# Unrotated scores of the latent attention from high and low halves: three one-record products in place of one of full operands

## Chip, cores and metric

One core of one Trainium2 chip. The metric is the device time of one execution in microseconds; the figure for the kernel before is the median of three runs. Times inside an execution are from one profiled execution.

## The reference

Two blocks in a row, in float32, on 512 tokens of width 2048. The first is a windowed attention block with sinks; the change does not touch it. The second puts 16 meta tokens ahead (528 keys), projects the normed tokens and runs two attentions, one differential (8 heads) and one latent (8 heads), gates both and projects back. The latent one is what the change touches:

```python
q_nope, q_pe = qB[..., :B_NOPE], _rope(qB[..., B_NOPE:], pos)      # 128 unrotated, 64 rotated
k_nope, vB = kvB[..., :B_NOPE], kvB[..., B_NOPE:]
s = (einsum('bhqd,bhkd->bhqk', qn, k_nope) + einsum('bhqd,bkd->bhqk', qp, k_pe)) * scale
s = where(rel >= 0, s, -inf);  p = softmax(s)
o = einsum('bhqk,bhkd->bhqd', p, v)
```

## The kernel before, in words

The kernel is written by hand, one instruction stream for each engine, synchronized by counting semaphores. Its backbone is a series of projections ("chunks"): 512 tokens (4 tiles of 128) times 16 blocks of 128 rows of a weight, 512 columns wide. A chunk has 64 steps; step Q is the product of token tile t = Q % 4 with weight block k = Q // 4. Both operands are split: a value x is held as hi (rounded to float32r) and lo = x - hi, also float32r, and one product is hi·hi + hi·lo + lo·hi, three matmuls of 512 columns (L601 to L603). A float32r matmul leaves one record in the trace; one of plain float32 operands leaves two. ScalarE makes the high half of each weight block (L1061), GpSimd the low half (L1559); SyncE loads the weights.

The attentions are interleaved with the steps of four chunks. The function attend_body (for TensorE at L947, ScalarE L1421, VectorE L2117; GpSimd's is attend_loads, L1685) says for each step Q what an engine issues besides the projection; the order of the work is written out by these step numbers, the same on each engine. Chunks 26 and 27 carry the latent attention (object MLA), four heads each; chunks 28 and 29 carry the differential one (DIFF). A head has four units, one for each 128 queries; unit u stands at step unit_time(u) = 12 + 3u (L441). Tile j of a head sees (j + 1)·128 + 16 keys: 144, 272, 400, 528, the last in two cuts of 272 and 256 because of the PSUM bank.

For a latent head, in the order of its work:

- GpSimd loads its q, k and v (load_qk L1645, load_v L1660) into one of two buffers. VectorE rotates the 64 rotated columns of q in place (rotate L2021) at step 12·head - 3, for head 0 at step 4.
- head_turn (L874) transposes at three steps, given by turn_time (L445): b = 0 the unrotated q, b = 1 the rotated q (with 64 unrotated columns beside it), b = 2 the unrotated k. All three go into the one PSUM bank turn[0], the 16 meta keys into turn[1]. For heads 1 to 3 the steps are 12·head + 2, + 5 and + 7; for head 0 they are 6, 8 and 10. b = 0 waits for the rotation.
- keep_head (L1376) on ScalarE copies them out: q to qnT (L1382, times the scale, float32), k to knT (L1388, L1390, float32); of the rotated q the high half to the upper 64 partitions of qpT (L1385). Of the latter VectorE writes the low half to the lower 64 partitions (L2134), so that one float32r product against a doubled k covers both halves.
- scores2 (L902) at the unit's step: for each cut, one product of qnT and knT in float32 (L917), then qpT against kpeT_hi and against kpeT_lo in float32r (L919, L920), all into the same PSUM region.
- soften2 (VectorE, L2086) adds the mask and takes the maximum in the same step; weigh2 (ScalarE, L1393) takes the exponential one step later; combine (VectorE, L2100) the reciprocal at + 2; turn_p2 (TensorE, L923) transposes p into turn[0] at + 3 (L929, L931); keep_pT2 (ScalarE, L1399) copies that out; values2 (TensorE, L934) at + 5 multiplies with v (L943, L944) into turn[1]; keep_o2 (VectorE, L2111) scales it out at + 5.

Who may write turn[0] is counted: each use (three turns and four p's a head) waits in t0_use (L897) until the semaphore A.free has as many releases as uses went before. The instruction that last reads the bank adds one: L1382 for b = 0, L2134 for b = 1, L1390 for b = 2, the end of keep_pT2 for p. values2 of the latent attention waits for all releases of the uses so far:

```python
pe.wait_ge(A.free, i * (4 * A.batches + NU) + ((count["t0"] if A.mla else turned_at[u]) + 1))
```

Within a step TensorE issues first the projection, then values2, head_turn, scores2, turn_p2. ScalarE: the weight split (each fourth step), weigh2, keep_head, keep_pT2. VectorE: keep_o2, combine, the rotation, the low half of q, soften2. Each queue is in order.

## Time and profile before

| What | Value |
|---|---|
| Median of three runs | 1683.43 us (1682.55 to 1684.44) |
| The profiled execution's own time | 1682.62 us |
| Its span, first to last instruction | 1680.8 us |
| Mean granted TensorE clock | 0.999 |
| TensorE busy | 1666.2 us (99%), 8383 matmul records |
| VectorE, ScalarE, GpSimd busy | 695.9 us (41%), 784.3 us (47%), 707.4 us (42%) |
| The two latent bodies | from 1048 to 1218 us |

Busy of TensorE counts from the start of a matmul to its modelled end, and matmuls are pipelined, so rows overlap; the distance between two starts is what a matmul takes of the engine. PE is TensorE, PEld its weight loads, DVE VectorE, ACT ScalarE, POOL GpSimd. The chain of waits follows the execution back from its last instruction to what released each step.

### The profile page before, as it was taken

How to read it: one execution, taken by the hardware profiler on the slowest of the kernel's cores; microseconds unless marked ns; L12 is line 12 of the kernel's file. 1: busy time of each engine (PE TensorE's matmuls, PEld its weight loads, DVE VectorE, ACT ScalarE, POOL GpSimd, SP SyncE). 2: the span in 40 equal slices, each digit the busy share in tenths (PEclk: the TensorE clock that was granted, in tenths of full speed). 3: DMA queues.
4: the chain of work that ended last, by engine and by line, in shares of the span. 5: the costliest groups of instructions: out<-in, count | busy, mean ns of one | idle time of the engine just before them, and what ended most of it. 6: DMA issues, size and time to landing. Idle time of an engine off the chain costs nothing.

```text
span 1680.8 us, 22142 instructions
## 1 busy us (share of the span) xinstructions
PE 1666.2 (99%) x8383; PEld 1367.0 (81%) x8383; DVE 695.9 (41%) x1696; ACT 784.3 (47%) x1699; POOL 707.4 (42%) x569
## 2 busy tenths in 40 slices
PE   9999999999999999999999999999999999999998
PEld 7889898888888888898887787888866767888886
DVE  4356656663135666231100001423234344767574
ACT  4356666664334455442312236444455555434551
POOL 4442433225666304455455544434333333665022
PEclk9999999999999999999999999999999999999999
DMA  6341444214886577433677676423332212324772
GB/s 228 115 125 51 128 84 116 76 56 125 195 182 145 168 237 252 142 122 125 129 209 190 181 195 224 144 93 120 104 114 89 95 51 76 99 79 142 237 245 100
DMA packets 118374, 234.81 MB, mean 140 GB/s; under 512 B 8475, under 2 KB 16220, under 8 KB 118124
## 3 DMA queue, kind: packets, MB, share of 16 engines
q1 hardware_dynamic: 78332, 147.70, 26.6%
q0 software_dynamic: 18352, 48.15, 13.9%
q10 hardware_dynamic: 21584, 37.55, 6.9%
q8 instruction: 67, 1.10, 0.3%
q14 instruction: 39, 0.32, 0.1%
HBM read 208.41 MB, written 58.51 MB: 159 GB/s over the span
## 4 chain that ended last, share of the span: by engine, by line
PE 94%; DVE 3%; issue 1%; ACT 1%; POOL 1%; DMA 0%; DVEq 0%; ACTq 0%; POOLq 0%
PE acc L601 21%; PE acc L603 20%; PE acc L602 20%; PE sc L917 4%; PE turn L698 3%; PE turn L943 2%; PE turn L623 2%; PE turn L686 1%; PE acc L741 1%; PE acc L742 1%; PE acc L743 1%; PE sc L614 1%; PE sc L615 1%; PE turn L931 1%; PE sc L673 1%
## 5 line engine op out<-in xcount | busy, mean ns | idle before, releaser
L1559 POOL TENSOR_TENSOR w_lo<-w_raw,w_hi 128x512 fp32r<-128x512 f32 x405 | 584.9, 1450 | 886.2 <-ACT w_hi L1061 875.8
L1061 ACT ACTIVATE w_hi<-w_raw 128x512 fp32r<-128x512 f32 x517 | 323.3, 628 | 497.3 <-PE acc L603 403.6
L601 PE MATMUL acc<-w_hi,setA_hi 128*128 128x512 f32 (+1 forms) x1344 | 544.2, 405 | 2.5 <-DVE setA_lo L1744 0.8
L603 PE MATMUL acc<-w_hi,setA_lo 128*128 128x512 f32 (+1 forms) x1344 | 521.0, 388 | 0.0
L602 PE MATMUL acc<-w_lo,setA_hi 128*128 128x512 f32 (+1 forms) x1344 | 519.6, 387 | 0.0
L601 PEld LDWEIGHTS acc<-w_hi,setA_hi 128*128 128x128 f32 x1344 | 252.8, 188 | 57.2 <-issue 11.7
L603 PEld LDWEIGHTS acc<-w_hi,setA_lo 128*128 128x128 f32 x1344 | 252.2, 188 | 53.0
L602 PEld LDWEIGHTS acc<-w_lo,setA_hi 128*128 128x128 f32 x1344 | 253.4, 189 | 40.0
L1912 DVE TENSOR_TENSOR w_lo<-w_raw,w_hi 128x512 fp32r<-128x512 f32 x112 | 78.7, 708 | 64.0 <-ACT w_hi L1061 63.9
L2016 DVE TENSOR_TENSOR sum_m<-sc,tmp_m 16x512 f32<-16x512 f32 (+1 forms) x9 | 5.9, 656 | 230.1 <-ACT tmp_m L1081 230.1
L1137 ACT ACTIVATE p_w<-sm,negm 128x256 f32<-128x256 f32 (+1 forms) x128 | 60.6, 474 | 57.1 <-DVE sink_d L1814 57.1
L1396 ACT ACTIVATE p<-sm,negm 128x144 f32<-128x144 f32 (+3 forms) x96 | 54.3, 566 | 53.5 <-DVE negm L2097 53.5
L917 PE MATMUL sc<-knT,qnT 64*128 64x272 f32 (+6 forms) x240 | 77.7, 415 | 0.8 <-DVE negm L2097 0.4
L601 PE MATMUL acc<-w_hi,setB_hi 128*128 128x512 f32 x192 | 76.7, 399 | 0.0
L603 PE MATMUL acc<-w_hi,setB_lo 128*128 128x512 f32 x192 | 75.0, 391 | 0.0
L602 PE MATMUL acc<-w_lo,setB_hi 128*128 128x512 f32 x192 | 74.8, 390 | 0.0
L1404 ACT ACTIVATE pT<-turn 128x128 f32<-128x128 f32 (+1 forms) x64 | 28.0, 437 | 91.7 <-PE turn L931 91.7
L698 PEld LDWEIGHTS turn<-vg,pT 128*128 128x128 f32 x448 | 59.9, 191 | 5.3
L917 PEld LDWEIGHTS sc<-knT,qnT 64*128 64x128 f32 (+1 forms) x240 | 39.3, 186 | 22.0 <-DVE negm L2097 13.0
L698 PE MATMUL turn<-vg,pT 128*128 128x64 f32 x448 | 56.9, 267 | 0.0
L2115 DVE TENSOR_SCALAR o_nat<-turn,rden 128x128 f32<-128x128 f32 x64 | 22.4, 349 | 81.3 <-PE turn L944 81.3
L1810 DVE CUSTOM_DVE_ANT_0 sm<-sc,bias,sink_g 128x256 f32<-128x256 f32 (+1 forms) x128 | 52.5, 447 | 0.1
(391 smaller groups left out, 2546.1 us busy)
## 6 DMA issues: line engine op xcount, KB each, us to landing
w_raw<-in_w_in SPq DMA_DIRECT2D x48, 1024.0 KB, 5.1
w_raw<-in_swa_w_in SPq DMA_DIRECT2D x35, 1024.0 KB, 7.5
w_raw<-sum_out SPq DMA_DIRECT2D x64, 256.0 KB, 3.8
sum_out<-in_swa_w_out POOLq DMA_DIRECT2D x24, 512.0 KB, 7.8
sum_out<-in_w_out POOLq DMA_DIRECT2D x24, 512.0 KB, 7.8
sum_out<-sum_out POOLq DMA_DIRECT2D x16, 512.0 KB, 6.7
w_raw<-in_swa_w_out SPq DMA_DIRECT2D x8, 1024.0 KB, 5.3
w_raw<-in_swa_w_out SPq DMA_DIRECT2D x24, 256.0 KB, 3.9
```

Source lines behind the costliest of these rows:

```text
L601: mm(acc[t][:, 0:cols], hi[:, kc, rows], wh, start=(k == 0), stop=False)
L602: mm(acc[t][:, 0:cols], hi[:, kc, rows], wl, start=False, stop=False)
L603: last = mm(acc[t][:, 0:cols], lo[:, kc, rows], wh, start=False, stop=(k == K - 1))
L623: last = nc.tensor.transpose(turn[bank][:, t * P:(t + 1) * P], tile, ident[:])
L698: last = mm(o_ps[:, h * HD:(h + 1) * HD], pT[:, u % 2, 2 * h + c], vg[:, j - 1 + c], start=(c == (1 if j == 0 else 0)), stop=(c == 1))
L917: last = mm(dst, qnT[rows, buf, q], knT[rows, buf, keys], start=True, stop=not A.mla)
L1061: nc.scalar.activation(w_at(f)[0], raw_of(f), ACT.Copy).then_inc(done, 1)
L1137: nc.scalar.activation(p_w[:, u % 2, h, first:], sm[:, u % 2, h, first:], ACT.Exp, bias=negm[:, u % 2, h:h + 1], scale=-1.0, accum_out=den ...
L1396: nc.scalar.activation(p2[:, u % 2, comp, lo:], sm2[:, slot, lo:], ACT.Exp, bias=negm_2[:, u % 2, comp:comp + 1], scale=-1.0, accum_out=de ...
L1559: nc.gpsimd.tensor_tensor(lo, raw_of(f), hi.bitcast(F32), ALU.subtract).then_inc(s_lo, 1)
L1810: last = V.tensor_tensor_reduce(sm[:, u % 2, h, first:], sc[h][:, first:256], bias[:, head, first:], -1.0, sink_g[:, head:head + 1], ALU.a ...
L1912: V.tensor_tensor(lo, raw_of(f), hi.bitcast(F32), ALU.subtract).then_inc(s_wlo, 1)
```

## The change

The unrotated q and k are no longer kept as float32 but as a high and a low half in float32r. ScalarE's copies (the same number of them) now write the high halves; VectorE writes the low halves by subtraction from PSUM, and it is VectorE that now releases turn[0] after b = 0 and b = 2. Each score cut has three float32r products for the unrotated part where it had one float32 product. The low halves lie in a part of SBUF that nothing uses at that time (qn_lo at B_LO, kn_lo behind it). For head 0 the turns stand at steps 4, 7, 10; b = 0 waits for the loads alone, and b = 1 for the rotation. The differential attention's part of the code is only rewritten.

```diff
@@ -209,8 +209,12 @@
         gate_0 = over("gate_0", [P, NT, CW], B_HI)
         nat_k = over("nat_k", [P, 2, NT, VD], B_HI + 6144)
         nat_v = over("nat_v", [P, 2, NT, VD], B_HI + 10240)
+        qn_hi = over("qn_hi", [P, 2, S], B_HI + 14336, F32R)
+        qn_lo = over("qn_lo", [P, 2, S], B_LO, F32R)
+        qpT = over("qpT", [P, 2, S], B_HI + 18432, F32R)
+        kn_hi = over("kn_hi", [P, 2, KEYS], B_HI + 22528, F32R)
+        kn_lo = over("kn_lo", [P, 2, KEYS], B_LO + 4096, F32R)
         qnT = over("qnT", [P, 2, S], B_HI + 14336)
-        qpT = over("qpT", [P, 2, S], B_HI + 18432, F32R)
         knT = over("knT", [P, 2, KEYS], B_HI + 22528)
         alibi = over("alibi", [P, ALIBI_AT[NT]], B_HI + 26752)
         kpeT_lo = over("kpeT_lo", [P, KEYS], B_HI + 29952, F32R)
@@ -312,7 +316,7 @@
         s_short = [sem(f"s_short{i}") for i in range(2)]
         s_st, s_gld, s_zero = sem("s_st"), sem("s_gld"), sem("s_zero")
         s_lam, s_alibi, s_fin_w, s_x1in, s_h2, s_fin = (sem("s_" + n) for n in ("lam", "alibi", "fin_w", "x1in", "h2", "fin"))
-        s_qp_hi = sem("s_qp_hi")
+        s_qp_hi, s_qn_hi, s_kn_hi = sem("s_qp_hi"), sem("s_qn_hi"), sem("s_kn_hi")
         s_km_in, s_km_ps, s_km = sem("s_km_in"), sem("s_km_ps"), sem("s_km")
         s_sum, s_sq, s_fin_last, s_x1last = sem("s_sum"), sem("s_sq"), sem("s_fin_last"), sem("s_x1last")
 
@@ -445,7 +449,7 @@
         def turn_time(A, head, b):
 
             if head == 0:
-                return 6 + 2 * b if A.mla else 5 + 3 * b
+                return 4 + 3 * b if A.mla else 5 + 3 * b
             return 12 * head + ((2, 5, 7)[b] if A.mla else (5, 8)[b])
 
         def score_at(A, u, comp):
@@ -875,7 +879,9 @@
 
                 buf, use = head % 2, i * 2 + (head // 2 + 1)
                 if b == 0:
-                    pe.wait_ge(A.rope if A.mla else A.ld_qk[buf], i * 4 + (head + 1) if A.mla else use * 32)
+                    pe.wait_ge(A.ld_qk[buf], use * (48 if A.mla else 32))
+                if A.mla and b == 1:
+                    pe.wait_ge(MLA.rope, i * 4 + (head + 1))
                 t0_use(A, i)
                 if b == A.batches - 1:
                     if A.mla:
@@ -914,8 +920,12 @@
                 for first, end in zip(cuts, cuts[1:]):
                     keys = slice(first, end)
                     dst = sc2[:, start + keys.start:start + keys.stop]
-                    last = mm(dst, qnT[rows, buf, q], knT[rows, buf, keys], start=True, stop=not A.mla)
-                    if A.mla:
+                    if not A.mla:
+                        last = mm(dst, qnT[rows, buf, q], knT[rows, buf, keys], start=True, stop=True)
+                    else:
+                        mm(dst, qn_hi[:, buf, q], kn_hi[:, buf, keys], start=True, stop=False)
+                        mm(dst, qn_lo[:, buf, q], kn_hi[:, buf, keys], start=False, stop=False)
+                        mm(dst, qn_hi[:, buf, q], kn_lo[:, buf, keys], start=False, stop=False)
                         mm(dst, qpT[:, buf, q], kpeT_hi[:, keys], start=False, stop=False)
                         last = mm(dst, qpT[:, buf, q], kpeT_lo[:, keys], start=False, stop=True)
                 last.then_inc(A.score, 1)
@@ -1377,18 +1387,22 @@
                 buf = head % 2
                 act.wait_ge(A.full, i * (4 * A.batches + NU) + (count["t0"] + 1))
                 count["t0"] += 1
-                scale = B_SCALE if A.mla else A_SCALE
+                if A.mla:
+                    if b == 0:
+                        nc.scalar.activation(qn_hi[:, buf], turn[0][:], ACT.Copy, scale=B_SCALE).then_inc(s_qn_hi, 1)
+                    elif b == 1:
+                        nc.scalar.activation(qpT[ROPE:P, buf], turn[0][ROPE:P, :], ACT.Copy, scale=B_SCALE).then_inc(s_qp_hi, 1)
+                    else:
+                        nc.scalar.activation(kn_hi[:, buf, META:KEYS], turn[0][:], ACT.Copy)
+                        nc.scalar.activation(kn_hi[:, buf, 0:META], turn[1][:, 0:META], ACT.Copy).then_inc(s_kn_hi, 1)
+                    return
                 if b == 0:
-                    last = nc.scalar.activation(qnT[:, buf], turn[0][:], ACT.Copy, scale=scale)
-                elif b < A.batches - 1:
-
-                    nc.scalar.activation(qpT[ROPE:P, buf], turn[0][ROPE:P, :], ACT.Copy, scale=scale).then_inc(s_qp_hi, 1)
-                    return
+                    last = nc.scalar.activation(qnT[:, buf], turn[0][:], ACT.Copy, scale=A_SCALE)
                 else:
+                    n = 4 * i + head
                     nc.scalar.activation(knT[:, buf, META:KEYS], turn[0][:], ACT.Copy)
-                    meta = turn[1][:, 0:META] if A.mla else diff_kmT[:, (4 * i + head) * META:(4 * i + head + 1) * META]
-                    last = nc.scalar.activation(knT[:, buf, 0:META], meta, ACT.Copy)
-                last.then_inc(A.free, 1)
+                    last = nc.scalar.activation(knT[:, buf, 0:META], diff_kmT[:, n * META:(n + 1) * META], ACT.Copy)
+                last.then_inc(DIFF.free, 1)
 
             def weigh2(A, i, u, comp):
                 lo, slot = S - (u % NT + 1) * P, u % 2 if A.mla else comp
@@ -2129,6 +2143,16 @@
                             x1, x2_ = nat_q[:, buf, :, VD:VD + HR], nat_q[:, buf, :, VD + HR:QB]
                             rotate((x1, x2_), (x1, x2_), cos[:], sin[:], [rope_t[:, n] for n in range(4)]).then_inc(MLA.rope, 1)
                             dve.wait_ge(MLA.rope, i * 4 + (head + 1))
+                        if A.mla and Q == turn_time(A, head, 0):
+                            dve.wait_ge(s_qn_hi, i * 4 + (head + 1))
+                            V.scalar_tensor_tensor(qn_lo[:, head % 2], turn[0][:], B_SCALE, qn_hi[:, head % 2].bitcast(F32),
+                                                   ALU.mult, ALU.subtract).then_inc(MLA.free, 1)
+                        if A.mla and Q == turn_time(A, head, 2):
+                            dve.wait_ge(s_kn_hi, i * 4 + (head + 1))
+                            V.tensor_tensor(kn_lo[:, head % 2, 0:META], turn[1][:, 0:META],
+                                            kn_hi[:, head % 2, 0:META].bitcast(F32), ALU.subtract)
+                            V.tensor_tensor(kn_lo[:, head % 2, META:KEYS], turn[0][:],
+                                            kn_hi[:, head % 2, META:KEYS].bitcast(F32), ALU.subtract).then_inc(MLA.free, 1)
                         if A.mla and Q == turn_time(A, head, 1):
                             dve.wait_ge(s_qp_hi, i * 4 + (head + 1))
                             V.scalar_tensor_tensor(qpT[0:ROPE, head % 2], turn[0][ROPE:P, :], B_SCALE,
```

## Rows read from the trace of the kernel before

**Rows 1.** Chain by engine; windows view: us, busy PE, PEld, DVE, ACT, POOL (count), PEclk, DMA, GB/s

```profile
PE 94%; DVE 3%; issue 1%; ACT 1%; POOL 1%; DMA 0%; DVEq 0%; ACTq 0%; POOLq 0%
...
1048.00:1218.00 170.00, 169.82 (x986) 142.27 (x985) 52.33 (x220) 75.78 (x202) 70.38 (x77) 1.00 0.36 114
```

**Rows 2.** Timeline of TensorE: start us, us, engine line op out<-in; scores of four widths

```profile
1066.47 0.83 PE L917 MATMUL sc<-knT,qnT 128*128 128x400 f32 x2
...
1067.33 0.34 PE L920 MATMUL sc<-kpeT_lo,qpT 128*128 128x400 f32 x1
1067.51 0.27 PE L929 MATMUL turn<-ident,p 128*16 128x128 f32 x1
...
1071.67 0.62 PE L917 MATMUL sc<-knT,qnT 128*128 128x272 f32 x2
...
1072.25 0.28 PE L920 MATMUL sc<-kpeT_lo,qpT 128*128 128x272 f32 x1
1072.37 0.59 PE L917 MATMUL sc<-knT,qnT 128*128 128x256 f32 x2
...
1072.92 0.29 PE L920 MATMUL sc<-kpeT_lo,qpT 128*128 128x256 f32 x1
1073.05 0.27 PE L929 MATMUL turn<-ident,p 128*16 128x128 f32 x1
...
1076.47 0.41 PE L917 MATMUL sc<-knT,qnT 128*128 128x144 f32 x2
...
1076.78 0.27 PE L920 MATMUL sc<-kpeT_lo,qpT 128*128 128x144 f32 x1
1076.89 0.27 PE L929 MATMUL turn<-ident,p 128*16 128x128 f32 x1
```

**Rows 3.** Waits view, 1048 to 1218 us: us in total, times, longest us

```profile
PEld turn L943 <- ACT knT L1390: 1.8, 6, 0.3
...
PEld turn L884 <- DVE qpT L2134: 1.0, 2, 0.5
```

**Rows 4.** Timeline after b2 of head 2, first body

```profile
1088.44 0.18 ACT L1390 ACTIVATE knT<-turn 128x16 f32<-128x16 f32 x1
...
1088.67 0.41 PEld L943 LDWEIGHTS turn<-nat_v,pT 128*128 128x128 f32 x3 [0.30 <-ACT knT L1390]
```

**Rows 5.** Timeline after b0 and after b1 of head 2, first body

```profile
1080.57 0.60 ACT L1382 ACTIVATE qnT<-turn 128x512 f32<-128x512 f32 x1 [1.79 <-PE turn L889]
1081.78 0.27 PE L929 MATMUL turn<-ident,p 128*16 128x128 f32 x1
...
1084.46 0.59 ACT L1385 ACTIVATE qpT<-turn 64x512 fp32r<-64x512 f32 x1 [0.81 <-PE turn L892]
1085.15 0.69 DVE L2134 SCALAR_TENSOR_TENSOR qpT<-turn,qpT 64x512 fp32r<-64x512 f32 x1 [0.71 <-ACT qpT L1385]
1085.99 0.27 PE L929 MATMUL turn<-ident,p 128*16 128x128 f32 x1
```

**Rows 6.** Groups by line: busy us, mean ns; timeline of VectorE, head 1's rotation

```profile
L1794 DVE TENSOR_TENSOR kT_lo<-turn,kT_hi 128x512 fp32r<-128x512 f32 x4 | 2.7, 677 | 0.0
...
L2059 DVE TENSOR_TENSOR kpeT_lo<-sc,kpeT_hi 64x16 fp32r<-64x16 f32 x2 | 0.3, 156 | 0.0
...
1059.46 0.29 DVE L2028 TENSOR_TENSOR nat_q<-rope_t 128x128 f32<-128x128 f32 x1
1059.67 0.28 DVE L2029 TENSOR_TENSOR nat_q<-rope_t 128x128 f32<-128x128 f32 x1
```

**Rows 7.** Source view of L884: duration ns min/median/max

```profile
L884 PE MATMUL turn<-ident,nat_k x64: 270/273/330, 1057.4 to 1382.1; 128*128 128x128 f32 x64
```

**Rows 8.** Timeline of head 0, first body, to its first scores

```profile
1057.66 1.36 DVE L2025 TENSOR_TENSOR rope_t<-nat_q,sin 128x128 f32<-128x128 f32 x1
...
1058.70 0.18 ACT L1390 ACTIVATE knT<-turn 128x16 f32<-128x16 f32 x1
...
1059.60 0.41 PE L917 MATMUL sc<-knT,qnT 128*128 128x144 f32 x2
```

## The prediction

> **What bounds the kernel now.** I read the chain of waits first: TensorE holds 94% of it [rows 1]. The windows view of the stretch that the change touches, the two latent-attention bodies (chunks 26 and 27, 1048 to 1218 us), shows TensorE busy for 169.8 of 170 us at the full clock, VectorE for 52, ScalarE for 76 [rows 1]. So each nanosecond of TensorE issue time there counts, and so does each wait in TensorE's in-order queue; work on VectorE or ScalarE costs nothing by itself, but where TensorE waits for its result it does. A matmul row's duration includes its drain, so a product costs the distance from its start to the next start. I took that from the timeline. Then I read the waits view and the timeline around the turns of a head, to find who waits for the one bank turn[0].
>
> Below, step +n is projection step 12·head+n of a body. With heads 1 to 3 the bank turn[0] is used in this order: p turned (+0), q unrotated (+2, "b0"), p (+3), q rotated (+5, "b1"), p (+6), k (+7, "b2"), p (+9). Values run at +5, +8 and so on. In the latent bodies values2 (L940) waits for as many releases as turn[0] has had uses, so the values at +8 wait for the release of b2.
>
> **The scores.** A full-operand product shows as two records, a one-record product as one. All distances are start to start, up to L929 or the next L917 [rows 2].
> - 144 keys: five records' unit takes 1076.47 to 1076.89 = 0.42 us, the last one-record product 0.11. Five one-record products: 0.55, so +0.13.
> - 272 keys: 1071.67 to 1072.37 = 0.70; one product 0.12; five 0.60, so -0.10. It occurs twice in a head (tile 1, and the first cut of tile 3).
> - 256 keys: 0.68; one product 0.13 by this row, five 0.65 at most; I take -0.06.
> - 400 keys: 1066.47 to 1067.51 = 1.04; one product 0.18; five 0.90, so -0.14.
> A head: 0.13 - 0.10 - 0.14 - 0.10 - 0.06 = -0.27. Eight heads: **-2.2 us**. The gain is small because at 144 keys a one-record product takes 0.11 us where its 144 columns are 0.06 at 2.4 GHz, the granted level there [rows 1]: I read it as the three products paying for their weight loads, which the long full-operand product hid.
> The Trainium skill says in FP8 and Floating Point Precision, TensorE Precision Notes, that true FP32 is 4 passes through the array. By that alone one pass over 1344 keys a head is saved, 0.56 us, or 4.5 us in all, an estimate; the 272 and 400 rows are near it, the 144 row is against it and decides here.
>
> **b2, the turn of k.** Now ScalarE copies k (L1388, L1390) and releases the bank; TensorE waits for precisely this: the waits view has 6 waits of the value products for L1390 [rows 3]. In the timeline L1390 ends at 1088.44 + 0.18 = 1088.62 and the weight load of L943 starts at 1088.67, 0.05 later [rows 4]. After the change the same two ScalarE copies write the high half, then VectorE makes two subtractions, and the last one releases. Added: 0.10 from the end of a ScalarE copy to VectorE's start (L1385 ends at 1085.05, L2134 starts at 1085.15 [rows 5]); the 16-column subtraction, 0.16 long, of which 0.07 lies under its successor, as with L2028 and L2029 (0.29 long, starts 0.21 apart): 0.09; and the 512-column one from PSUM, 0.68 [rows 6]. Sum 0.87, bounds 0.78 (the small one free) to 0.95. TensorE already waits there, so all of it lands on the path: 6 x 0.87 = **+5.2 us**. Behind the subtraction in VectorE's queue stand keep_o2 and combine of step +8, which need the delayed values anyway.
>
> **b0, the turn of q unrotated.** Now L1382 ends at 1080.57 + 0.60 = 1081.17 and L929 of the p turned at +3 starts at 1081.78, so there is 0.61 of cover [rows 5]. After: 1081.17 + 0.10 + 0.69 (as L2134, same shape of operation on 64 rows) = 1081.96, and 0.05 to TensorE: 1082.01. The scores before it are 0.10 shorter, so L929 would be due at 1081.68. Wait 0.33, and a first transpose after a wait takes 0.06 more (330 against 273 ns [rows 7]): 0.39 x 6 = **+2.3 us**. Bounds: 0.23 (if the shorter scores count for nothing and the restart is free) to 0.5.
>
> **b1, the turn of q rotated.** Nothing is added, but its cover shrinks. L2134 ends at 1085.84, TensorE could go on at 1085.89; L929, now at 1085.99, would be due at 1085.85 with the 400-key scores 0.14 shorter [rows 5]. 0.04 + 0.06 = 0.10, six times: **+0.6 us**. So most of the 400-key gain is given back.
>
> **Head 0 of each body.** The turns move from steps 6, 8, 10 to 4, 7, 10; b0 no longer waits for the rotation, which b1 does. The loads landed before the rotation that ran ahead of step 6, and three steps of some 0.7 us between turns cover the longer chain. The wait of b2 for L2134 goes (1.0 us over 2 by the load side's idle time [rows 3]). In its place comes a later k: the scores at step 12 now start at 1059.60, after L1390 ends at 1058.88 [rows 8]. After: in VectorE's queue the rotation of head 1 (step 9) stands ahead of k's subtraction (step 10). It ends at 1059.67 + 0.28 = 1059.95 [rows 6]; everything up to it comes a step earlier, 1059.25; then 0.05 + 0.09 + 0.68 and 0.05: 1060.12, that is +0.5. In that rotation one operation, L2025, took 1.36 us where its like take 0.28 [rows 6, 8]; without that the result is about nothing. I take +0.25 each, **+0.5 us** (-0.1 to +1.1).
>
> Nothing else is on the path. ScalarE runs as many copies as before, of the same lengths. VectorE gets three more subtractions a head, some 1.5 us against 118 idle; POOL only waits longer before it loads a head that is used 12 steps on. No transfer is added.
>
> **Sum.** -2.2 + 5.2 + 2.3 + 0.6 + 0.5 = +6.4 us. The profiled execution took 1682.62 us (span 1680.8 and 1.8 around it) and would become 1689.0. It lies 0.8 under the median of the runs; on the median 1683.43 + 6.4 = **1689.8 us**.
>
> **Rivals.**
> 1. *The release is hidden*: turn[0]'s subtraction runs under projection steps, as it does for head 0's b1, and TensorE's waits do not grow. For: VectorE is two thirds idle. Against: the 6 waits for L1390, and cover of 0.61 against a chain of 0.84 at b0. It decides at the values of step +8: if they don't wait for k's low half, 5.2 goes and 1684.6 is left; if b0 is covered as well, 1681.7. Not slower. Chance 0.10.
> 2. *A whole pass is saved*: every full-operand product costs four passes and every one-record product one, also at 144 keys, by a weight load that is hidden. Then -4.5 in place of -2.2, with the waits as above: 1687.5. This is the page's rule named above. Against: 0.11 us steps of one-record products at 144 keys. Chance 0.04; together with rival 1 (1683.4 - 4.5 = 1678.9, faster) 0.03.
> 3. *Knock-on*: VectorE's queue, which now holds the subtractions with their waits for ScalarE, delays the softmax of the next unit, mostly where the rotation (up to 1.4 us long in one operation) follows at +9, and p comes late to its turn. 6 x 0.7 = 4 us more: 1694. Against: the unit's turn is three steps, over 3 us, behind its scores. Chance 0.08.
> The forecast keeps 0.75.
>
> **Range and chances.** The bounds of b2 (±0.5), b0 (-1.0, +0.7), head 0 (±0.6), the scores (-2.3 by rival 2) and of the runs' own spread give 1686.3 to 1692.8; rival 1 and most of rival 3 stay out. About 0.2% (3.4 us) can be told from no change here. Faster needs rivals 1 and 2 together: 0.03. Within 0.2%: rival 1 and its kin, 0.12. Slower: 0.85.
>
> **What would show it.** In the waits view of the changed kernel: 6 waits of value products (L943's successor) for the subtraction that makes kn_lo, each about 0.9 us longer than the 6 for L1390 now; 6 of the turned p at +3 for qn_lo, about 0.35 each; 2 at step 12 for kn_lo. The four tile widths should show 0.55, 0.60, 0.90 and 1.2 to 1.25 us in scores. If the value products at +8 start as early as now, the forecast is wrong at its largest term. If one-record products of 144 keys step at 0.06, the second term is wrong.

## The result, and the profile after

The changed kernel took 1692.24 us (median of 5 runs, 1691.63 to 1692.85) against 1683.43 for the kernel before (1682.52 to 1684.61): a ratio of 1.0054 [1.0043, 1.0065], so 0.5% slower, clear of the runs' spread. The forecast was 1689.8 with a range from 1686.3 to 1692.8. The sign was right, and so were the waits behind it; the change costs 8.8 us where 6.4 were forecast, and the time lies 0.6 us inside the upper end of the range.

First the page and two windows views, which cut out the two latent bodies, from the first product of chunk 26 to the transposes of `diff_km` (start and end, length, busy time of PE, PEld, DVE, ACT and POOL with counts, granted clock, DMA share, GB/s). The kernel before:

```profile
1048.60:1218.70 170.10, 169.92 (x985) 142.09 (x984) 52.68 (x221) 75.37 (x201) 69.78 (x77) 1.00 0.36 115
```

The kernel after, its page and the same stretch:

```profile
span 1689.8 us, 22254 instructions
...
PE 92%; DVE 4%; issue 1%; ACT 1%; POOL 1%; DVEq 0%; POOLq 0%; ACTq 0%
...
1048.94:1228.00 179.06, 170.11 (x1026) 143.88 (x1024) 65.49 (x245) 75.46 (x201) 69.80 (x77) 1.00 0.35 109
```

The bodies grew by 8.96 us, which is the whole change of the span (+9.0). TensorE's busy time in them is the same (169.92 and 170.11), so the new time is idle time: 0.18 us of it before, 8.95 after. (The cheaper scores don't show in the busy time: before a wait, the 0.39 us row of the last product counts as busy, of which 0.16 lies beyond its 0.23 us step.) The chain shows it as 2% less of TensorE and 1% more of VectorE [rows 1]. VectorE, with 12.8 us more work, is far from full; it costs only as the last link before TensorE.

**The scores.** Timeline of TensorE after, two widths (start, duration, engine, line, operation):

```profile
1080.30 0.23 PE L926 MATMUL sc<-kn_hi,qn_hi 128*128 128x144 f32 x1
1080.36 0.27 PE L927 MATMUL sc<-kn_hi,qn_lo 128*128 128x144 f32 x1
1080.47 0.28 PE L928 MATMUL sc<-kn_lo,qn_hi 128*128 128x144 f32 x1
...
1080.81 0.27 PE L939 MATMUL turn<-ident,p 128*16 128x128 f32 x1
...
1069.71 0.35 PE L926 MATMUL sc<-kn_hi,qn_hi 128*128 128x400 f32 x1
1069.90 0.34 PE L927 MATMUL sc<-kn_hi,qn_lo 128*128 128x400 f32 x1
...
1070.45 0.34 PE L930 MATMUL sc<-kpeT_lo,qpT 128*128 128x400 f32 x1
1070.70 0.27 PE L939 MATMUL turn<-ident,p 128*16 128x128 f32 x1
```

The 144-key tile takes 1080.30 to 1080.81 = 0.51 us where it took 0.42 [rows 2]: slower, as forecast, though the first product is only 0.06 from the next. The 400-key tile steps at 0.185: five are 0.92, against 1.04. Of 272 keys 0.70 became 0.63, of the last tile's 528 in two cuts 1.38 became 1.22. A head: +0.09 - 0.07 - 0.12 - 0.16 = -0.26, eight heads **-2.1 us**.

**Who waits for k's low half.** Waits view of 1048 to 1226 us (total us, times, longest), and the timeline around b2 of head 2, first body; the line numbers of L943, L1388 and L1390 have become L953, L1396 and L1397:

```profile
PEld turn L953 <- DVE kn_lo L2154: 6.7, 6, 1.1
PEld sc L926 <- DVE kn_lo L2154: 4.5, 2, 3.0
...
1092.59 0.39 PE L607 MATMUL acc<-w_hi,setA_lo 128*128 128x512 f32 x1
1092.62 0.18 ACT L1397 ACTIVATE kn_hi<-turn 128x16 fp32r<-128x16 f32 x1
...
1092.83 0.17 DVE L2152 TENSOR_TENSOR kn_lo<-turn,kn_hi 128x16 fp32r<-128x16 f32 x1 [1.86 <-ACT kn_hi L1397]
1092.92 0.68 DVE L2154 TENSOR_TENSOR kn_lo<-turn,kn_hi 128x512 fp32r<-128x512 f32 x1
...
1093.65 0.52 PEld L953 LDWEIGHTS turn<-nat_v,pT 128*128 128x128 f32 x4 [1.11 <-DVE kn_lo L2154]
```

The six weight loads of the values waited 0.3 us for ScalarE's copy [rows 3, 4]; now they wait 1.1 us for the subtraction. From the last projection product to the values is 1.06 us, before 0.27; over the six places the difference is 0.79 to 0.81 us, together **+4.8**. The chain in it: ScalarE's copy ends at 1092.80, 0.03 to VectorE, 0.09 for the 16 columns, 0.68 for the 512 (to 1093.60), and the 0.05 to the weight load that were there before.

**Waits for q.** The same view of the timeline, b0 of head 2, first body:

```profile
1084.49 0.60 ACT L1392 ACTIVATE qn_hi<-turn 128x512 fp32r<-128x512 f32 x1 [1.79 <-PE turn L895]
...
1085.19 0.69 DVE L2148 SCALAR_TENSOR_TENSOR qn_lo<-turn,qn_hi 128x512 fp32r<-128x512 f32 x1 [0.72 <-ACT qn_hi L1392]
...
1085.49 0.28 PE L930 MATMUL sc<-kpeT_lo,qpT 128*128 128x272 f32 x1
...
1085.99 0.27 PE L939 MATMUL turn<-ident,p 128*16 128x128 f32 x1 [0.21 <-issue]
```

From L930 to L939 is 0.49 to 0.50 us, where without a wait it is 0.12 [rows 2]: 0.37 each, six times **+2.2**. The waits view names no releaser for it:

```profile
PEld turn L939 <- issue: 4.2, 14, 0.4
```

The sign that the prediction had set, six waits of the turned p for qn_lo, thus can't be read in that view. That it is this wait rests on the times (qn_lo ends at 1085.88, L939 starts at 1085.99) and on q_low_left_out below. At b1 the same distance is 0.25 against 0.18 before (1070.45 to 1070.70 above, behind head 1's b1): 0.07 each, **+0.4**.

**Head 0.** VectorE, GpSimd and TensorE in the first body, timeline of the kernel after:

```profile
1055.33 3.79 POOL L1573 TENSOR_TENSOR w_lo<-w_raw,w_hi 128x512 fp32r<-128x512 f32 x3
1056.92 2.35 DVE L2038 TENSOR_TENSOR rope_t<-nat_q,cos 128x128 f32<-128x128 f32 x1
...
1059.88 1.26 POOL L1573 TENSOR_TENSOR w_lo<-w_raw,w_hi 128x512 fp32r<-128x512 f32 x1 [0.77 <-ACT w_hi L1071]
1059.91 1.38 DVE L2042 TENSOR_TENSOR nat_q<-rope_t 128x128 f32<-128x128 f32 x1
1061.21 0.28 DVE L2043 TENSOR_TENSOR nat_q<-rope_t 128x128 f32<-128x128 f32 x1
1061.53 0.17 DVE L2152 TENSOR_TENSOR kn_lo<-turn,kn_hi 128x16 fp32r<-128x16 f32 x1
1061.62 0.68 DVE L2154 TENSOR_TENSOR kn_lo<-turn,kn_hi 128x512 fp32r<-128x512 f32 x1
1062.35 0.33 PE L926 MATMUL sc<-kn_hi,qn_hi 128*128 128x144 f32 x1 [2.61 <-DVE kn_lo L2154]
```

And the last of GpSimd's subtractions there, in the kernel before:

```profile
1059.91 1.29 POOL L1559 TENSOR_TENSOR w_lo<-w_raw,w_hi 128x512 fp32r<-128x512 f32 x1 [1.03 <-ACT w_hi L1061]
```

ScalarE had k's high half by 1058.87. The low half stands in VectorE's queue behind the rotation of head 1 (L2038 to L2043), and that takes 4.6 us: two of its six operations last 2.35 and 1.38 us where the others take 0.28, one under each of GpSimd's stretches. From the start of the body to the first scores it is 13.41 us against 11.00 (1048.60 to 1059.60 [rows 8]). In the second body two operations take 0.73 and 1.36, and the same distance grew from 10.93 to 11.78. Together **+3.3**.

Counted from the body's start, GpSimd's first stretch stands where it stood (6.39 us in, 6.38 before), but its second comes 0.37 earlier (10.94 in place of 11.31). It follows ScalarE's copy of the weight block, which follows TensorE's projection steps, and with head 0's turns moved TensorE reaches the first product of step 12 after 9.95 us and not 10.31. Before, the last operation of the rotation started 0.24 us ahead of that second subtraction (1059.67 [rows 6]) and took 0.28; now L2042 starts 0.03 behind it and is held for 1.1.

The sum of what was read: -2.1 + 4.8 + 2.2 + 0.4 + 3.3 = +8.6, against 8.96 in the bodies. Of the 0.4 left, 0.2 stands at the first tile of head 0: behind its wait it takes 0.62 us and not 0.51 (1062.35 to 1062.97, and the same in the second body).

### The profile page after: what moved, and what is told of

Same layout as the page of the kernel before. It is cut to its first block, busy times and chain, and to the rows that moved or that the text cites. A ratio compares the mean times of both kernels' runs of the same rounds, so it can differ in the third digit from the quotient of the medians.

```text
span 1689.8 us, 22254 instructions
## 1 busy us (share of the span) xinstructions
PE 1667.3 (99%) x8423; PEld 1369.3 (81%) x8423; DVE 708.9 (42%) x1720; ACT 784.6 (46%) x1699; POOL 708.8 (42%) x569
## 4 chain that ended last, share of the span: by engine, by line
PE 92%; DVE 4%; issue 1%; ACT 1%; POOL 1%; DVEq 0%; POOLq 0%; ACTq 0%
PE acc L605 20%; PE acc L607 20%; PE acc L606 20%; PE sc L924 3%; PE turn L702 3%; PE turn L953 2%; PE turn L627 2%; PE turn L690 1%; PE acc L745 1%; PE acc L747 1%; PE acc L746 1%; PE sc L618 1%; PE sc L619 1%; PE turn L941 1%; PE sc L677 1%
## 5 line engine op out<-in xcount | busy, mean ns | idle before, releaser
L605 PE MATMUL acc<-w_hi,setA_hi 128*128 128x512 f32 (+1 forms) x1344 | 544.3, 405 | 2.4 <-DVE setA_lo L1758 0.7
L607 PE MATMUL acc<-w_hi,setA_lo 128*128 128x512 f32 (+1 forms) x1344 | 521.0, 388 | 0.0
L605 PEld LDWEIGHTS acc<-w_hi,setA_hi 128*128 128x128 f32 x1344 | 252.8, 188 | 57.2 <-issue 11.7
L607 PEld LDWEIGHTS acc<-w_hi,setA_lo 128*128 128x128 f32 x1344 | 252.2, 188 | 53.2
L605 PE MATMUL acc<-w_hi,setB_hi 128*128 128x512 f32 x192 | 76.7, 399 | 0.0
L607 PE MATMUL acc<-w_hi,setB_lo 128*128 128x512 f32 x192 | 75.0, 391 | 0.0
L953 PEld LDWEIGHTS turn<-nat_v,pT 128*128 128x128 f32 x320 | 45.0, 190 | 11.5 <-DVE kn_lo L2154 6.7
L924 PE MATMUL sc<-knT,qnT 64*128 64x272 f32 (+3 forms) x160 | 53.1, 428 | 0.4
```

What stands on the lines that cost most here:

```text
L605: mm(acc[t][:, 0:cols], hi[:, kc, rows], wh, start=(k == 0), stop=False)
L607: last = mm(acc[t][:, 0:cols], lo[:, kc, rows], wh, start=False, stop=(k == K - 1))
L924: last = mm(dst, qnT[rows, buf, q], knT[rows, buf, keys], start=True, stop=True)
L953: mm(dst, pT2[:, u % 2, b * P:(b + 1) * P], nat_v[:, buf, b], start=(b == 0), stop=False)
```

## The experiments

The change's ratio is against the 1683.43 above, each other one against runs of the kernel before on the same chip as the run (medians 1682.86 to 1682.88). Each trace is of one execution, so a body is one execution's. "Body" is the stretch cut as above; before 170.10, after 179.06. The last two columns are differences from the kernel before, in us.

| run | median us | ratio, 95% | body us | median over before | body over before |
|---|---|---|---|---|---|
| the change | 1692.24 | 1.0054 [1.0043, 1.0065] | 179.06 | +8.8 | +9.0 |
| k_meta_first | 1686.96 | 1.0024 [1.0015, 1.0033] | 174.62 | +4.1 | +4.5 |
| rotate_after_k | 1688.90 | 1.0035 [1.0023, 1.0048] | 176.36 | +6.0 | +6.3 |
| both_waits | 1683.30 | 1.0004 [0.9995, 1.0012] | 170.62 | +0.4 | +0.5 |
| products_only | 1681.40 | 0.9992 [0.9983, 1.0001] | 168.57 | -1.5 | -1.5 |
| no_pool_lows | 1689.00 | 1.0038 [1.0024, 1.0053] | 176.41 | +6.1 | +6.3 |
| q_low_left_out | 1692.33 | 1.0054 [1.0041, 1.0067] | 176.80 | +9.5 | +6.7 |
| p0_one_later | 1681.07 | 0.9990 [0.9981, 0.9999] | 168.42 | -1.8 | -1.7 |
| head0_turns_back | 1690.13 | 1.0044 [1.0031, 1.0057] | 178.06 | +7.3 | +8.0 |
| before_meta_first | 1683.00 | 1.0001 [0.9992, 1.0010] | 169.26 | +0.1 | -0.8 |
| p0_full_product | 1683.65 | 1.0002 [0.9993, 1.0011] | 170.08 | +0.8 | 0.0 |

**k_meta_first.** From the change: k's 16 meta columns are copied and subtracted ahead of its 512, and the values wait for those and for their own turned p, no longer for the newest use of turn[0].

```
-                pe.wait_ge(A.free, i * (4 * A.batches + NU) + ((count["t0"] if A.mla else turned_at[u]) + 1))
+                pe.wait_ge(A.free, i * (4 * A.batches + NU) + (turned_at[u] + 1))
+                if A.mla:
+                    pe.wait_ge(MLA.slope, 4 * i + count["k"])
...
-                        nc.scalar.activation(kn_hi[:, buf, META:KEYS], turn[0][:], ACT.Copy)
-                        nc.scalar.activation(kn_hi[:, buf, 0:META], turn[1][:, 0:META], ACT.Copy).then_inc(s_kn_hi, 1)
+                        nc.scalar.activation(kn_hi[:, buf, 0:META], turn[1][:, 0:META], ACT.Copy).then_inc(MLA.w, 1)
+                        nc.scalar.activation(kn_hi[:, buf, META:KEYS], turn[0][:], ACT.Copy).then_inc(s_kn_hi, 1)
```

> The changed kernel, but of k the 16 meta columns (bank turn[1]) are copied and subtracted first, with a signal of their own, and the value products wait for that and for their own p, no longer for the release of turn[0]. Theory A (the six value products at step +8 stand 0.85 us too long for k's low half, behind 0.15 that they stood before too): all six waits go, 6 x 0.95 = 5.7 us less than the changed kernel, 1686.5 us. Theory B (the longer time is the products' own or VectorE's load): no wait of the value products matters, 1692 us, within 1 us.

Measured: 1686.96, 4.7 us of the 8.8 gone. TensorE at b2 of head 2 (L956 and L957 are the values here), timeline, and the windows view of the first body:

```profile
1092.92 0.40 PE L607 MATMUL acc<-w_hi,setA_lo 128*128 128x512 f32 x1
1093.15 0.60 PE L956 MATMUL turn<-nat_v,pT 128*128 128x128 f32 x4
1093.60 0.39 PE L957 MATMUL turn<-natm_v,pTm 128*128 128x128 f32 x2
1093.74 0.47 PE L605 MATMUL acc<-w_hi,setA_hi 128*128 128x512 f32 x1
...
1048.77:1062.40 13.63, 11.02 (x55) 8.66 (x53) 9.78 (x21) 5.57 (x10) 9.02 (x11) 1.00 0.75 245
1062.40:1066.40 4.00, 4.00 (x16) 3.37 (x16) 0.47 (x4) 0.61 (x3) 2.03 (x3) 0.59 0.51 141
```

L607 to the next step's L605 is 0.82 us; in the change it is 1092.59 to 1094.34 = 1.75. So 0.93 is saved at each of six places, 5.6 us. Only 4.4 show in the body, because in this kernel the granted clock fell to the lower of its two levels (1.2 GHz) for 3.4 us from 1063.09, soon after TensorE's 2.6 us of idling before head 0's first scores: 0.59 over 4.00 us is (1 - 0.59) x 4.00 = 1.6 us lost. All ten runs show a mean granted clock of 0.997 or 0.998, so the loss isn't of this one execution alone. The change idles as long at the same place and keeps the full clock in its trace. With the 1.6 added back the edit gives 6.0 to 6.1 us; what it has over 5.6 is for the most part the wait before the second body's first scores, 1.10 us from L607 to the scores in place of 1.38. So the values' wait is the largest term, as forecast.

**rotate_after_k.** From the change: head 1's rotation moved from step 9 to step 11 of VectorE's order, behind k's subtraction at step 10.

```
-                        if A.mla and Q == max(12 * head - 3, 4):
+                        if A.mla and Q == (4, 11, 21, 33)[head]:
```

> The changed kernel, but the rotation of head 1's q stands on VectorE at step 11, behind k's low half of head 0 (step 10), in place of step 9. Theory A (the waits of 3.0 and 1.4 us before head 0's first scores are k's subtraction queued behind that rotation): they shrink to 0.35 and 0.45, gap before the first scores, so 2.7 + 0.9 = 3.6 us less, 1688.6 us. Theory B (head 0 waits because its three turns stand closer, or because its loads come late): no change, 1692.2 us.

Measured: 1688.90; body -2.7. VectorE of the first body, timeline:

```profile
1058.88 0.68 DVE L2154 TENSOR_TENSOR kn_lo<-turn,kn_hi 128x512 fp32r<-128x512 f32 x1
...
1059.88 1.37 DVE L2040 TENSOR_TENSOR rope_t<-nat_q,sin 128x128 f32<-128x128 f32 x1
...
1063.46 0.69 DVE L2148 SCALAR_TENSOR_TENSOR qn_lo<-turn,qn_hi 128x512 fp32r<-128x512 f32 x1 [0.39 <-ACT qn_hi L1392]
...
1064.25 0.27 PE L939 MATMUL turn<-ident,p 128*16 128x128 f32 x1 [0.67 <-issue]
```

The low half of k is ready at 1059.56, and the distance from L607 to the first scores (0.23 us without a wait) falls from 3.01 us to 0.38. But the rotation, still held up once (1.37 us), now comes ahead of head 0's first softmax (1062.02) and, behind it, of the subtraction for head 1's q, and TensorE waits 0.47 us more at that turn in each body (L930 to L939 0.96 in place of 0.49). This is the third rival's knock-on in small.

**both_waits.** Both edits above.

> Both of the two edits before at once. Theory A: the two are different waits and add up, 5.7 + 3.6 = 9.3 us less than the changed kernel, 1682.9 us, which is no different from the kernel before. Theory B (one wait moves into the next): less than the sum, 1685 us or more.

Measured: 1683.30, body 170.62: -8.4, against -6.1 (4.4 and the 1.6 of clock) and -2.7 alone, so the two add up to within 0.4 us. Of 9.0 us 0.5 is left. In the waits view the values no longer stand; before head 0's scores 0.7 us of load-side waiting is left in two waits, and the waits of the turned p behind b0 are all still there. So what the scores gain goes into those waits.

**products_only.** From the kernel before: three one-record products of the high halves, no low halves made.

```
-                    last = mm(dst, qnT[rows, buf, q], knT[rows, buf, keys], start=True, stop=not A.mla)
-                    if A.mla:
+                    if not A.mla:
+                        last = mm(dst, qnT[rows, buf, q], knT[rows, buf, keys], start=True, stop=True)
+                    else:
+                        for n in range(3):
+                            mm(dst, qn_hi[:, buf, q], kn_hi[:, buf, keys], start=(n == 0), stop=False)
```

> The kernel before, with three one-record products of the high halves in place of the full-operand product, and no low halves: the unrotated part is three times high by high, so the low halves are left out of the result. The releases stay with ScalarE's copies. Theory A (the products themselves gain 2.1 us, as the starts in the changed kernel show: 144 keys +0.09, 272 -0.07, 400 -0.11, 528 -0.17, a head -0.26): 2.1 less than before minus some 0.4 that the shorter cover of the rotated q gives back, 1681.7 us. Theory B (a whole pass of four is saved everywhere): 4.5 less, 1678.9 us. Theory C (the products gain nothing, weight loads eat it): 1683.4 us.

Measured: 1681.40, body -1.5. The interval of the ratio just includes 1; it is the body that shows the gain. So with the releases as before, the products alone save 1.5 us and not 4.5: the 2.1 read above, less what the shorter cover of b1 takes back (0.4). The second rival, the whole pass saved, falls. The change thus loses by everything it adds around the products.

The profiled execution took 1682.94, 1.5 over the median, and lost it before any changed instruction: the bodies start at 1050.43. Timeline of TensorE at the program's start:

```profile
9.03 0.63 PE L605 MATMUL acc<-w_hi,setA_lo 128*128 128x512 f32 x1
9.45 0.63 PE L603 MATMUL acc<-w_hi,setA_hi 128*128 128x512 f32 x1
```

Here 512-column products step at 0.43 us, up to 10.73, where at the full clock they step at 0.23.

**no_pool_lows.** From the change: GpSimd writes one column in place of 512 in the low halves of the first eight weight blocks of chunk 26.

```
-                    nc.gpsimd.tensor_tensor(lo, raw_of(f), hi.bitcast(F32), ALU.subtract).then_inc(s_lo, 1)
+                    n = 1 if B[26] <= f < B[26] + 8 else CW
+                    nc.gpsimd.tensor_tensor(lo[:, 0:n], raw_of(f)[:, 0:n], hi[:, 0:n].bitcast(F32), ALU.subtract).then_inc(s_lo, 1)
```

> The changed kernel; for the first 8 weight blocks of chunk 26 GpSimd subtracts one column in place of 512, so the low halves of these weights are left out. Theory A (VectorE's operations of two SBUF inputs in the rotation, 2.4 and 1.4 us where 0.28 is usual, stand still while GpSimd's w_lo subtraction runs): the rotation of head 1 in the first body takes 1.4 us in place of 4.6, ends before k's high half is there, and the wait before the first scores falls from 3.0 to about 0.4; the second body keeps its 1.4 us wait. 2.6 us less than the changed kernel: 1689.6 us. Theory B (the rotation waits for head 1's load or for DMA traffic): its operations stay long, 1692.2 us.

Measured: 1689.00, body -2.65. VectorE, timeline (L2039 to L2044 are the rotation here):

```profile
1055.60 0.69 DVE L2159 SCALAR_TENSOR_TENSOR qpT<-turn,qpT 64x512 fp32r<-64x512 f32 x1 [1.55 <-ACT qpT L1394]
1056.32 0.31 DVE L2039 TENSOR_TENSOR rope_t<-nat_q,cos 128x128 f32<-128x128 f32 x1
...
1057.48 0.28 DVE L2044 TENSOR_TENSOR nat_q<-rope_t 128x128 f32<-128x128 f32 x1
1058.37 0.17 DVE L2153 TENSOR_TENSOR kn_lo<-turn,kn_hi 128x16 fp32r<-128x16 f32 x1 [0.61 <-ACT kn_hi L1397]
```

With GpSimd out of the way the same six operations take 1.44 us in all, not 4.6, and the subtraction follows right on ScalarE's copy. In the second body, where GpSimd's work was left as it is, two operations still take 0.69 and 1.36 us. So GpSimd's subtractions, not the data or the queue, hold up the rotation.

**q_low_left_out.** From the change: the subtraction for qn_lo is left out, ScalarE's copy releases the bank, and qn_hi stands in for qn_lo.

```
-                        mm(dst, qn_lo[:, buf, q], kn_hi[:, buf, keys], start=False, stop=False)
+                        mm(dst, qn_hi[:, buf, q], kn_hi[:, buf, keys], start=False, stop=False)
...
-                        nc.scalar.activation(qn_hi[:, buf], turn[0][:], ACT.Copy, scale=B_SCALE).then_inc(s_qn_hi, 1)
+                        nc.scalar.activation(qn_hi[:, buf], turn[0][:], ACT.Copy, scale=B_SCALE).then_inc(MLA.free, 1)
```

> The changed kernel without q's low half: ScalarE's copy of the high half releases turn[0], and the second product takes the high half once more. The number of products is the same. Theory A (the p turned at +3 waits 0.37 us for that release in heads 1 to 3 of both bodies, and in head 0 it costs nothing): 6 x 0.37 = 2.2 us less than the changed kernel, 1690.0 us. Theory B (the longer distance ahead of L939 is what a transpose after five one-record products costs, with no wait): 1692.2 us.

Measured: 1692.33, no better than the change, which by the median alone speaks for the rival theory. The trace tells otherwise: L930 to L939 at b0 is back at 0.12 us and the body is 2.26 shorter, 6 x 0.38. The time went at the start of the program. Windows view of this kernel, then of the change:

```profile
8.40:11.60 3.20, 3.20 (x9) 2.48 (x8) 0.75 (x1) 2.24 (x4) 2.38 (x2) 0.50 1.07 381
```

```profile
8.40:11.60 3.20, 3.20 (x18) 2.63 (x17) 0.75 (x1) 2.14 (x5) 2.96 (x3) 1.00 1.05 382
```

For 3.4 us, long before any changed instruction, TensorE ran at half its clock (9 products where the other did 18), and (1 - 0.50) x 3.20 = 1.6 us were lost; the bodies start at 1050.60 and not 1048.94. The profiled execution took 1691.43; without the 1.6 it would be 1689.8. Its five runs stand between 1690.65 and 1692.62, all at a mean granted clock of 0.997 or 0.998 (the change's at 0.998 or 0.999); where the four that have no trace lost theirs isn't known. The forecast of 1690.0 is missed by the median; the b0 term is borne out by the body.

**head0_turns_back.** From the change: the turns of head 0 at steps 6, 8, 10 again.

```
-                return 4 + 3 * b if A.mla else 5 + 3 * b
+                return 6 + 2 * b if A.mla else 5 + 3 * b
```

> The changed kernel with head 0's turns back at steps 6, 8 and 10. Theory A (a turn with its subtraction holds turn[0] for some 1.7 us, two steps cover 1.5): two waits of about 0.3 a body come back, and the rotation of head 1 starts up to 0.7 later, so the wait before the first scores is as long or longer: 0.5 to 2 us more, 1692.7 to 1694.2 us. Theory B (the moved turns are what makes head 0 wait): less than the changed kernel, 1690 us.

Measured: 1690.13, a miss on the other side: 1.5 us less over before than the change has. The expected waits came (0.24 us of idling at b1, then b2), but the distance from L607 to the first scores fell from 3.01 to 1.20 us, in the second body from 1.38 to 0.90. VectorE, timeline:

```profile
1057.40 1.24 DVE L2038 TENSOR_TENSOR rope_t<-nat_q,cos 128x128 f32<-128x128 f32 x1
...
1059.48 0.28 DVE L2043 TENSOR_TENSOR nat_q<-rope_t 128x128 f32<-128x128 f32 x1
1059.80 0.17 DVE L2152 TENSOR_TENSOR kn_lo<-turn,kn_hi 128x16 fp32r<-128x16 f32 x1
```

Counted from the body's start (1048.36 here, 1048.94 in the change) the rotation began 9.04 us in and not 7.98, while GpSimd's first stretch stood where it was (6.38 and 6.39). It met only that stretch's end (1.24 us, not 2.35) and was through before the second, which with TensorE waiting again came at 1059.97, 11.61 in and not 10.94. So the earlier turns, which are part of the change, cost more by this collision than they save in waits: the body is 1.0 us shorter without them.

**p0_one_later.** From both_waits: p of each head's first tile is turned one step later, when q's subtraction is done, and its copy stands ahead of the softmax on ScalarE.

```
+        def turn_at(A, u):
+
+            return unit_time(u) + A.turn_after + (1 if A.mla and u % NT == 0 else 0)
...
-                        if Q == unit_time(u) + A.turn_after:
+                        if Q == turn_at(A, u):
```

> The kernel both_waits, and the p of each head's first tile is turned at step +4 in place of +3, its copy ahead of the exponential on ScalarE. Theory A (turn[0]'s release after q's turn is all that is waited for at +3, so one more step of cover of 0.69 us takes the wait away, and the value products at +5 then wait about 0.1 for p's copy): 6 x 0.27 = 1.6 us less than both_waits, 1681.7 us, which would be 1.2 under the kernel before. Theory B (the wait only moves to the value products at +5): no change against both_waits, 1683.3 us.

Measured: 1681.07 in 11 runs, ratio 0.9990 [0.9981, 0.9999], body 168.42. TensorE after the 272-key tile of head 0, behind head 1's b0 (L935 is the tile's last product, L944 the turn of p), timeline:

```profile
1063.45 0.29 PE L935 MATMUL sc<-kpeT_lo,qpT 128*128 128x272 f32 x1
1063.57 0.39 PE L609 MATMUL acc<-w_hi,setA_hi 128*128 128x512 f32 x1
...
1064.45 0.27 PE L944 MATMUL turn<-ident,p 128*16 128x128 f32 x1
```

The projection's next step fills the wait. This is 1.8 us (0.1%) under the kernel before and 10.6 under the change, counted each against the kernel before: the best version found, though the gain over the kernel before is small. Its slowest run (1681.48) is below the fastest of the kernel before beside it (1682.48).

**before_meta_first.** From the kernel before: the 16 meta columns are copied first, and the values wait for those and for their own p, as in k_meta_first.

```
+                    if A.mla:
+                        nc.scalar.activation(knT[:, buf, 0:META], turn[1][:, 0:META], ACT.Copy).then_inc(MLA.slope, 1)
+                        nc.scalar.activation(knT[:, buf, META:KEYS], turn[0][:], ACT.Copy).then_inc(MLA.free, 1)
+                        return
```

> The kernel before, with k's 16 meta columns copied first and the value products waiting for them and their own p alone. Theory A (the wait of 0.15 us that six value products have for k's copy in the kernel before goes): the two latent bodies take 0.9 us less than the 170.1 of the kernel before, 1682.0 us. So of what p0_one_later gains, only the rest, 0.8 us, is owed to the one-record products with their later p. Theory B (that wait is paid for elsewhere): 170.1, 1682.9 us.

Measured: 1683.00, ratio 1.0001 [0.9992, 1.0010]; body 169.26, -0.84. From the last projection product to the next step's first is 0.82 us in place of 0.96 at each of the six places, 0.15 each. The median doesn't show it. By the bodies, 0.8 of the 1.7 us that p0_one_later gains could be had without the change.

**p0_full_product.** From p0_one_later: one full-operand product in place of the three; the low halves are made, but not used.

```
-                        mm(dst, qn_hi[:, buf, q], kn_hi[:, buf, keys], start=True, stop=False)
-                        mm(dst, qn_lo[:, buf, q], kn_hi[:, buf, keys], start=False, stop=False)
-                        mm(dst, qn_hi[:, buf, q], kn_lo[:, buf, keys], start=False, stop=False)
+                        mm(dst, qn_hi[:, buf, q].bitcast(F32), kn_hi[:, buf, keys].bitcast(F32), start=True, stop=False)
```

> The kernel p0_one_later with one full-operand product of the high halves in place of the three one-record products; the low halves are still made but used nowhere, so the unrotated part is from high halves alone. Theory A (the three products are worth 0.26 us a head, 2.1 us in all, also there): 1.7 to 2.1 more than p0_one_later, 1683.0 us, bodies of 170.3. Theory B (in that schedule something else covers the scores): no change, 1681.1 us.

Measured: 1683.65; body 170.08, 1.66 more than p0_one_later, so the products are worth 1.66 us where nothing waits. The medians differ by 2.6, of which the start of the program may hold a part.

## Why the prediction was right, point by point

- **The scores, -2.2**: measured -2.1 in the trace, -1.5 in products_only and -1.7 between p0_one_later and p0_full_product. That 144-key tiles lose was right: four of the five products step at 0.11 us. (The 0.42 us unit before has four records, not five as written; the sum isn't touched.) The reading behind it, that they pay for their weight loads, fits (the weight-load rows of the one-record products are 0.19 us long at all widths) but was not separated by a run.
- **b2, +5.2**: measured 6 x 0.80 = 4.8. The chain was as worked out but for the hand-over from ScalarE to VectorE, 0.03 in place of 0.10. Undone alone it gives back 5.6 by the distances, since it also takes away the 0.15 that stood there before.
- **b0, +2.3**: measured 6 x 0.37 = 2.2, and 2.26 in the body when q's subtraction is left out. Wait and restart were not quite split as I had them: the added 0.06 for the first transpose after a wait did not show (0.11 from L939 to the next, with a wait or without), the wait was longer by as much.
- **b1, +0.6**: measured 6 x 0.07 = 0.4, again without the restart.
- **Head 0, +0.5 (-0.1 to +1.1)**: measured **+3.3**. This is the mis-sized term, and more than the whole miss: the other terms come to 5.3 against 5.9. The place was named, the mechanism too: "in VectorE's queue the rotation of head 1 (step 9) stands ahead of k's subtraction". What failed is the sentence behind it, "everything up to it comes a step earlier". The forecast took the long L2025 [rows 8] along as it was, at most one of 1.36 us. But its length was not its own: it was that of GpSimd's subtraction running beside it. From the body's start the rotation was to end 10.65 us in (1059.25) and ended 12.55 in (1061.49), 1.9 late. It did begin 0.75 earlier (7.98 in place of 8.73), but GpSimd's first stretch did not move, so its first operation was held to the end of that stretch (2.35 us) and the 0.75 were lost. The other 1.1 us are the second subtraction (1.38 us for L2042), which the kernel before just missed and which the change itself brought 0.37 nearer. no_pool_lows shows this cause: without GpSimd's work the rotation takes 1.44 us in all. The step should have asked what an instruction that takes 1.36 us where its like take 0.28 is waiting for, and where that one stands after the move.
- **Rivals.** 1, the release hidden: fell: the six values wait 1.1 us each for the release, and b0 was not covered either. 2, a whole pass saved: fell by products_only. The Trainium skill's rule of 4 passes for true FP32 (FP8 and Floating Point Precision, TensorE Precision Notes) gave 4.5 us, an estimate; the trace disagrees, 2.1 were there, 1.5 to 1.7 of them in the bodies. 3, the knock-on through VectorE's queue at +9: not in heads 1 to 3, where the softmax came in time (the p turned after the 528-key and after the 144-key tiles follows the last product by 0.11 to 0.12 us, as before; 1080.69 to 1080.81 at head 2); its kin, the rotation ahead of k at head 0, is what was under-priced.
- **The range.** 1692.24 lies inside it, and in part by luck: head 0 came 2.2 us above its own upper bound, the other terms together 0.6 below their forecasts, and the upper end was 3.0 us above the forecast. The lower end is not the plain sum of the bounds either: 1689.8 - 0.5 - 1.0 - 0.6 - 2.3 is 1685.4, and 1686.3 was stated.
- The sum, +8.6 from the parts, stands within 0.4 of the 8.96 in the bodies; 0.2 of that is the slower first tile of head 0 in each body, the rest was not traced to a place.

What stays open: values that wait for their own p alone, and q's subtraction split in column halves, were not tried; so whether the last 0.5 us of both_waits could go without moving the turn of p isn't known. Why the granted clock fell in k_meta_first and not in the change is open too, and so is why a rotation operation that starts beside one of GpSimd's subtractions is let in right behind it in one place (the kernel before, 1057.33) and held over the next as well in another (the change, 1056.92).

## What to carry to other kernels

Splitting an operand into high and low halves adds a second engine's pass between the transpose's bank and its release, and where TensorE already waits for that bank the whole of it lands on the path: here 7.4 us of waits for 2.1 us of cheaper products. Order the releases first (the small copy whose bank is wanted ahead of the large one, each reader waiting for its own use alone, the next turn one step later), then make the split: with the first two and the rotation moved it came out even with the kernel before, with the later turn as well 0.1% below it. When a step is moved, look for its operations that last several times as long as their like: they are waiting for another engine, and the move changes what they meet.

## What the hardware showed that I had not expected

- **VectorE stands still beside GpSimd.** A 128x128 tensor-tensor operation with both inputs in SBUF took 0.28 us alone, and 0.41 to 2.35 us when it started while GpSimd's subtraction of a weight block ran (0.73, 1.36, 1.38 and 2.35 in the change); it then ended some 0.15 to 0.23 us after the end of one of those subtractions. An operation that had started before GpSimd's was not held (rotate_after_k's L2039, 0.28 us). The subtractions that read one input from PSUM took 0.68 to 0.69 us each time. This agrees with the Trainium skill, SBUF — State Buffer, Who interferes with whom, by which a VectorE instruction with two SBUF inputs contends with a GpSimd instruction that reads SBUF, and one with a single SBUF input does not; the size of the hold-up, up to 2.1 us, is from these traces.
- **TensorE's pace at the program's start differs from one profiled execution to another.** 3.4 us at half level from 8.3 us on cost q_low_left_out 1.6 us, in instructions that no kernel here changes. In products_only the same products stepped at 0.43 us up to 10.73 though the windows view prints a granted clock of 1.00 there: the steps themselves have to be read. Medians of whole runs hid an edit of 0.8 us and one of 2.3, which the stretch cut out of the trace shows.
- **A 144-column one-record product isn't always 0.11 us.** As the first behind a 512-column one it steps at 0.06 (1080.30 to 1080.36), the four that follow at 0.11 to 0.12.
